# Queries of a latent attention: 18 matmuls per slab step in place of 24, with the weights regathered and the rotation done on VectorE

## The chip, the cores and the metric

The kernel runs on one core of a Trainium2 chip. Its time is the device time of one execution in microseconds (us), the median of three runs where nothing else is said.

## The reference, cut to what matters

The reference is two transformer layers' worth of work, on 256 tokens of width 1024. The part that is changed is the last attention, a latent one with 16 heads. Queries have 64 plain columns ("nope") and 32 columns that are rotated by the token's position ("rope"). All heads share one rotated key of 32 columns.

```
c_q = rmsnorm(xn @ w_dq, cq_norm)                              # 768 wide
q = (c_q @ w_uq).reshape(B, S, 16, 64 + 32)
q = concatenate([q[..., :64], rope(q[..., 64:], positions)])
k = concatenate([k_nope, broadcast(k_rope, 16 heads)])
# rope: out = [x1 * cos - x2 * sin, x1 * sin + x2 * cos]
s = (q . k) / sqrt(96), causal softmax, times v, @ w_o
```

## The kernel before, in words

Everything is kept with features on the partitions and the 256 tokens on the free axis. The weights come as 319 slabs of 128 x 1024 numbers (512 KB), one after the other, through a ring of six slots in SBUF (`stage`). Each slab is split in two: ScalarE copies it to `w_hi` in the reduced format fp32r (`split_hi`, L787), and VectorE subtracts to get the rest, `w_lo` (`minus_hi`, L1141). TensorE then makes three matmuls for each 128 x 128 block: hi by hi, hi by lo, lo by hi (`by_weights`). A slab of eight blocks is 24 matmuls.

Each engine runs its own list of instructions in order, and all of them are written as a loop over the slabs. ScalarE splits slab n + 6 once TensorE has finished slab n (`next_hi`), VectorE splits slab n + 4 at its step n (`next_lo`), and the DMA queue reloads a slot when VectorE has split it. Beside the slabs each engine does in its step n what `attend(n)` gives it: the softmax of the attention heads.

The stage around the change is this. Nine slabs (DQ and KVA) make the latents; at the end of them VectorE rotates the shared key (`k_rope`). Two slabs (UK) make the keys and two (UV) the values. ScalarE's queue then sends the rotated key to all heads by DMA (`rope_keys`). Twelve slabs (UQ) make the queries; I number their steps s = 0 to 11. Eight slabs (MLAO) project the output.

Before the change a head has 128 query columns in UQ: 64 plain, 32 to rotate, and the same 32 with their halves exchanged. One VectorE multiplication by `rQ` takes each head out of PSUM; `rQ` holds the norm's factor, in its lower rows already multiplied by the cosine and the sine. The key carries its rotated 32 rows twice, so the product of 128 rows is the rotated score.

Head g has its scores at the end of step s = 1 + g (`mla_scores`, L594 and after), in steps 1 to 16. After them comes a round trip: VectorE adds the mask and finds the maximum (`maxima`, L1208, L1258), ScalarE takes the exponential (`exps`, L902), VectorE divides by the sum (`probs`, L1264, L1266) as the first thing of its next step, and TensorE transposes the result at the end of that next step (`turned`, L497). ScalarE copies it back (L909). Every second step ends with the product with the values (`outputs`), and its result is taken out by L913 on ScalarE and L1141 on VectorE. In TensorE's list the scores of head g stand ahead of the transposition of head g - 1, and they wait for the maximum of head g - 1.

## Time and profile before

| | |
|---|---|
| median of 3 runs | 1037.84 us (1036.15 to 1038.17) |
| the profiled execution | 1035.64 us, of which the span from first to last instruction is 1033.9 us |
| granted TensorE clock | 0.996 of full speed |
| TensorE busy | 1016.0 us (98%) |
| VectorE busy | 661.0 us (64%) |
| ScalarE busy | 556.8 us (54%) |
| the twelve UQ steps | 749.1 to 798.2 us |

The profile's busy time counts an instruction from its start to its end, and instructions that follow each other closely overlap. So the distance from one start to the next is what an instruction costs in a full queue, and I use that distance below. TensorE's weight loads (PEld) have sharper starts than its matmuls, and I time TensorE by them.

### The profile page before, as it was taken

The numbers are of one execution on the slowest core, as the hardware profiler recorded it, in microseconds if no ns is written. First come the engines' busy times: TensorE is split into PE (matmuls) and PEld (weight loads), VectorE is DVE, ScalarE is ACT, GpSimd is POOL, SyncE is SP. The second block draws the span as 40 slices with busy tenths as digits, with TensorE's granted clock in tenths as the row PEclk, the third lists the DMA queues.
The fourth block names the chain that finished last, engine by engine and source line by source line (L and its number), as shares of the span: only waits on it lengthen the run. The fifth ranks groups of instructions, "written<-read, shape, count | busy, mean of one in ns | idle before, by whom it ended". The sixth has DMA issues, their size and how long they took to land.

```text
span 1033.9 us, 21970 instructions
## 1 busy us (share of the span) xinstructions
PE 1016.0 (98%) x8296; PEld 989.5 (96%) x8296; DVE 661.0 (64%) x1219; ACT 556.8 (54%) x947; POOL 54.7 (5%) x76
## 2 busy tenths in 40 slices
PE   7999999999999999999999999999999999999997
PEld 7999899999999999999999999999999899999996
DVE  5545987775555558666476565648877676565654
ACT  6566786564444446565564444448566564444443
POOL 2021000120000002000010000002100020000000
PEclk9999999999999999999999999999999999999999
DMA  9634344466555555334455555555653445646531
GB/s 342 224 126 143 122 144 159 147 205 197 168 194 172 193 171 181 108 123 145 142 173 183 180 184 180 183 182 166 208 170 109 137 142 185 202 163 200 166 122 41
DMA packets 49208, 172.76 MB, mean 167 GB/s; under 512 B 5376, under 2 KB 7680, under 8 KB 49024
## 3 DMA queue, kind: packets, MB, share of 16 engines
q1 hardware_dynamic: 48096, 170.93, 49.5%
q10 hardware_dynamic: 1056, 1.05, 0.5%
q8 instruction: 39, 0.64, 0.3%
q14 instruction: 17, 0.14, 0.0%
HBM read 169.86 MB, written 1.05 MB: 165 GB/s over the span
## 4 chain that ended last, share of the span: by engine, by line
PE 93%; DVE 4%; ACT 2%; DMA 0%; issue 0%; POOLq 0%; SPq 0%; POOL 0%; ACTq 0%; DVEq 0%
PE bank L307 91%; DVE w_lo L1141 1%; PE bank L497 1%; DVE a_lo L1153 1%; DVE arena_r L1153 1%; DMA xT<-xT_dram 0%; ACT w_hi L787 0%; DVE xT L1170 0%; DVE arena L1134 0%; DVE tmp L1134 0%; ACT L973 0%; DVE arena L1400 0%; ACT soft_p L877 0%; ACT a_hi L827 0%; DVE arena L1388 0%
## 5 line engine op out<-in xcount | busy, mean ns | idle before, releaser
L787 ACT ACTIVATE w_hi<-stage 128x1024 fp32r<-128x1024 f32 x319 | 334.3, 1053 | 189.4 <-PE bank L307 186.0
L307 PE MATMUL bank<-a_hi,w_hi 128*128 128x256 f32 x1488 | 425.6, 287 | 8.2 <-ACT a_hi L987 7.4
L307 PE MATMUL bank<-a_hi,w_lo 128*128 128x256 f32 x1488 | 420.1, 283 | 0.0
L307 PE MATMUL bank<-a_lo,w_hi 128*128 128x256 f32 x1488 | 415.0, 283 | 0.0
L1141 DVE TENSOR_TENSOR w_lo<-stage,w_hi 128x1024 fp32r<-128x1024 f32 x319 | 387.2, 1230 | 10.5 <-ACT w_hi L787 10.3
L307 PE MATMUL bank<-arena_r,w_hi 128*128 128x256 f32 x1840 | 337.1, 285 | 0.8 <-DVE arena_r L1153 0.7
L307 PEld LDWEIGHTS bank<-a_hi,w_hi 128*128 128x128 f32 x1488 | 286.4, 192 | 12.3 <-DVE w_lo L1141 7.9
L307 PEld LDWEIGHTS bank<-arena_r,w_hi 128*128 128x128 f32 x1840 | 286.9, 192 | 2.5 <-DVE arena_r L1153 0.9
L307 PEld LDWEIGHTS bank<-a_hi,w_lo 128*128 128x128 f32 x1488 | 286.4, 192 | 0.0
L307 PEld LDWEIGHTS bank<-a_lo,w_hi 128*128 128x128 f32 x1488 | 283.3, 192 | 1.3 <-issue 1.2
L307 PE MATMUL bank<-arena_r,w_lo 128*128 128x256 f32 x920 | 259.3, 283 | 0.0
L307 PEld LDWEIGHTS bank<-arena_r,w_lo 128*128 128x128 f32 x920 | 176.4, 192 | 0.0
L1134 DVE TENSOR_TENSOR tmp<-bank,rB 128x256 f32<-128x256 f32 x66 | 28.0, 424 | 158.4 <-PE bank L307 158.4
L966 ACT ACTIVATE tmp<-tmp 128x256 f32<-128x256 f32 x66 | 27.6, 417 | 116.0 <-DVE tmp L1134 115.9
L959 ACT ACTIVATE arena_r<-tmp 128x256 fp32r<-128x256 f32 x66 | 27.6, 418 | 97.4 <-DVE tmp L1134 97.4
L1592 POOL TENSOR_TENSOR sumsq<-sumsq,sq 128x256 f32<-128x256 f32 x48 | 38.1, 793 | 718.9 <-ACT sq L813 606.4
L1134 DVE TENSOR_TENSOR tmp<-bank,tmp 128x256 f32<-128x256 f32 x66 | 28.0, 425 | 60.5 <-PE bank L307 60.2
L307 PE MATMUL bank<-w_hi,a_hi 128*128 128x256 f32 x128 | 37.9, 296 | 0.0
L307 PE MATMUL bank<-w_hi,a_lo 128*128 128x256 f32 x128 | 36.7, 287 | 0.0
L307 PE MATMUL bank<-w_lo,a_hi 128*128 128x256 f32 x128 | 36.7, 287 | 0.0
L902 ACT ACTIVATE soft_p<-soft_s,small 128x128 f32<-128x128 f32 x64 | 28.5, 448 | 12.4 <-DVE small L1258 12.1
L1134 DVE TENSOR_TENSOR arena<-bank,rB 128x256 f32<-128x256 f32 x44 | 18.4, 421 | 25.4 <-PE bank L307 25.3
(151 smaller groups left out, 720.5 us busy)
## 6 DMA issues: line engine op xcount, KB each, us to landing
stage<-slab_dram SPq DMA_DIRECT2D x319, 512.0 KB, 3.5
con<-con_dram SPq DMA_DIRECT2D x1, 1153.5 KB, 10.9
xT<-xT_dram SPq DMA_DIRECT2D x4, 256.0 KB, 5.3
arena<-arena ACTq DMA_DIRECT2D x2, 512.0 KB, 7.9
out_dram<-arena SPq DMA_DIRECT2D x8, 128.0 KB, 2.0
vec<-vec_dram SPq DMA_DIRECT2D x1, 245.5 KB, 3.7
pos<-pos_dram SPq DMA_DIRECT2D x1, 128.0 KB, 10.7
```

The lines of the kernel that those rows point to most:

```text
L307: return nc.tensor.matmul(out, lhsT, rhs, start=start, stop=True, skip_group_check=True)
L497: last = nc.tensor.transpose(b[:, i * P:(i + 1) * P], probs[:, i * P:(i + 1) * P], ident)
L787: nc.scalar.activation(w_hi[:, slot, :], stage[:, slot, :], ACT.Copy).then_inc(hi_made, 1)
L902: last = nc.scalar.activation(soft_p[:, g % 2, cols], soft_s[:, g % 2, cols], ACT.Exp, scale=soft_scale(g), bias=s_neg[:, i:i + 1], accum_ ...
L959: nc.scalar.activation(ff_hi[:, c // 2, :], tmp[:, 4 + c // 2, :], ACT.Copy).then_inc(ffhi_ready, 1)
L966: nc.scalar.activation(tmp[:, 2 + p, :], tmp[:, p, :], ACT.Silu).then_inc(silu_ready, 1)
L1134: return nc.vector.tensor_tensor(out, a, b, ALU.mult)
L1141: return nc.vector.tensor_tensor(out, a, hi.bitcast(f32), ALU.subtract)
L1153: return nc.vector.scalar_tensor_tensor(out, x, g, hi.bitcast(f32), ALU.mult, ALU.subtract)
L1592: nc.gpsimd.tensor_tensor(sumsq[:, :], sumsq[:, :], sq[:, (i % 2) * TOK:(i % 2 + 1) * TOK], ALU.add).then_inc(sq_added, 1)
```

## The change

The slabs in DRAM stay as they are, but ScalarE and VectorE read only 96 of the 128 columns of each head. They read three slabs (four heads) as one group, and write the split blocks regathered: the first six blocks of 128 columns hold the 32 rope columns of all four heads, the next six the 64 plain columns of heads 0 and 1, the last six those of heads 2 and 3. A step s is now one such part (`g, part = divmod(s, 3)`), of six blocks.

VectorE takes the rope part out twice for each head, once multiplied by the cosine and once by the sine. ScalarE takes the plain part out by two copies for each pair of heads. The norm's factor is no longer put on the queries; it is the scale of the exponential, one number per token in `rq_col`, and `rq_neg` for the maximum. The key's lower rows hold two different versions of the rotated key, made by eight VectorE instructions in place of four. An empty slab (GAP, 8 columns wide) makes the groups begin at slot 0. Cosine and sine are two tables of 128 rows, so there is one more Sin on ScalarE, in the first feed-forward.

```diff
-UQ = UV + 2
+GAP = UV + 2
+UQ = GAP + 1
...
-        def uq_out(h):
-            return half((4, 0, 1, 2)[h % 4], 0)
+        ROPE_BANK = 4
+
+        def uq_group(t, g):
+
+            return t[:, 3 * (g % 2):3 * (g % 2) + 3, :].rearrange("p s n -> p (s n)")
+
+        def uq_raw(h):
+
+            raw = uq_group(stage, h // 4).rearrange("p (b c) -> p b c", c=P)[:, 6 * (h % 4):6 * (h % 4) + 6, :]
+            return raw[:, :, 0:64], raw[:, :, 64:96]
+
+        def uq_split(t, h):
+
+            blocks = uq_group(t, h // 4)[:, 0:18 * P].rearrange("p (b c) -> p b c", c=P)
+            pair = 6 + 6 * (h % 4 // 2)
+            return (blocks[:, pair:pair + 6, 64 * (h % 2):64 * (h % 2) + 64],
+                    blocks[:, 0:6, 32 * (h % 4):32 * (h % 4) + 32])
...
-            load_rounds(fox + 4, rounds, (0, 1, 2, 3, 4, 5))
+            load_rounds(fox + 4, GAP // SLOTS, (0, 1, 2, 3, 4, 5))
+            for n in range(GAP // SLOTS * SLOTS, UQ):
+                sp.wait_ge(lo_made, n + 1 - SLOTS)
+                cols = slice(0, 8 if n == GAP else SLAB)
+                sp.dma_start(stage[:, n % SLOTS, cols], slab_d[n, :, cols]).then_inc(loaded[n % SLOTS], 16)
+            load_rounds(UQ // SLOTS, rounds, (-1, 0, 1, 2, 3, 4))
...
-                last.then_inc(slab_done, 1)
+                last.then_inc(slab_done, 2 if e == 3 else 1)
...
+                    norm_cols(rQ, latr_ready, 2, bank[7][:, 258:260], latcol_done)
-                n = UQ + s
-                if s == 0:
-                    pe.wait_ge(rope_ready, 1)
-                pe.wait_ge(lo_made, n + 1)
-                for j in range(8):
-                    h, b = divmod(8 * s + j, 6)
-                    if b == 0 and h == 1:
-                        pe.wait_ge(uv_taken, 2)
-                    if b == 0 and h == 3:
-                        pe.wait_ge(uk_taken, 2)
-                    if b == 0 and h >= 4:
-                        pe.wait_ge(uq_taken, h - 3)
-                    last = by_weights(n % SLOTS, j * P, uq_out(h), cq_hi[:, b, :], cq_lo[:, b, :],
-                                      b == 0)
-                last.then_inc(slab_done, 1)
-                attend(n)
+                g, part = divmod(s, 3)
+                if part == 0:
+
+                    pe.wait_ge(lo_made, UQ + 3 * g + 3)
+                    if g:
+                        pe.wait_ge(uq_rope, 4 * g)
+                    else:
+                        pe.wait_ge(rope_ready, 2)
+                    out = half(ROPE_BANK, 0)
+                else:
+
+                    i = 2 * g + part - 1
+                    pe.wait_ge(*((uv_taken, 2), (uv_taken, 2), (uk_taken, 2))[i] if i < 3 else (uq_nope, 2 * i - 4))
+                    out = half(i % 3, 0)
+                for b in range(6):
+                    w = slice((6 * part + b) * P, (6 * part + b + 1) * P)
+                    hi, lo = uq_group(w_hi, g)[:, w], uq_group(w_lo, g)[:, w]
+                    mm(out, hi, cq_hi[:, b, :], b == 0)
+                    mm(out, hi, cq_lo[:, b, :], False)
+                    last = mm(out, lo, cq_hi[:, b, :], False)
+                if part:
+                    last.then_inc(slab_done, part)
+                else:
+                    last.then_inc(uq_rope_done, 1)
+                attend(UQ + s)
...
+            def uq_split_hi(g, heads):
+                act.wait_ge(slab_done, (UK + 2, UV + 2, UQ + 3, UQ + 6)[g])
+                for j in heads:
+                    h, n = 4 * g + j, UQ + 3 * g + (0, 1, 2, 2)[j]
+                    act.wait_ge(loaded[n % SLOTS], 16 * (n // SLOTS + 1))
+                    (nope, rope), (nope_hi, rope_hi) = uq_raw(h), uq_split(w_hi, h)
+                    nc.scalar.activation(nope_hi, nope, ACT.Copy).then_inc(uq_hi, 1)
+                    nc.scalar.activation(rope_hi, rope, ACT.Copy).then_inc(hi_made if j else uq_hi, 1)
...
-                                                scale=soft_scale(g), bias=s_neg[:, i:i + 1],
-                                                accum_out=s_sum[:, i:i + 1])
+                                                scale=0.125 if g < HEADS else rq_col[:, t:t + 1],
+                                                bias=s_neg[:, i:i + 1], accum_out=s_sum[:, i:i + 1])
...
-                            nc.scalar.activation(trig[64:128, :], soft_s[64:128, 0, 0:TOK], ACT.Sin
-                                                 ).then_inc(trig_ready, 1)
+                            nc.scalar.activation(cosine[:, :], soft_s[:, 0, 0:TOK], ACT.Sin).then_inc(trig_ready, 1)
+                            nc.scalar.activation(sine[:, :], soft_s[:, 1, 0:TOK], ACT.Sin).then_inc(trig_ready, 1)
...
-                act.wait_ge(rope_ready, 1)
-                for r in (64, 96):
-                    nc.scalar.dma_start(mla_k[r:r + 32, :, :],
-                                        k_rope[64:96, :].unsqueeze(1).to_broadcast([32, HEADS, TOK])
-                                        ).then_inc(krope_ready, 16)
+                act.wait_ge(rope_ready, 2)
+                nc.scalar.dma_start(mla_k[64:128, :, :],
+                                    k_rope[64:128, :].unsqueeze(1).to_broadcast([64, HEADS, TOK])
...
+                if e:
+                    uq_split_hi(e // 3, ((0, 1), (2, 3), (0, 1))[e - 1])
+            def uq_nope_out(g, part):
+                n, i = UQ + 3 * g, 2 * g + part - 1
+                act.wait_ge(slab_done, n + 2 * part - 1)
+                for e in range(2):
+                    nc.scalar.activation(mla_q[0:64, 2 * i + e, :], half(i % 3, 0)[64 * e:64 * e + 64, :], ACT.Copy
+                                         ).then_inc(uq_nope, 1)
+                for m in range(n + part - 1, n + 2 * part - 1):
+                    next_hi(m)
+
+            uq_split_hi(1, (2, 3))
             for s in range(12):
-                next_hi(UQ + s)
+                if s % 3:
+                    uq_nope_out(*divmod(s, 3))
+                if s in (2, 5):
+                    uq_split_hi(2 + s // 3, (0, 1))
+                if s in (3, 6):
+                    uq_split_hi(1 + s // 3, (2, 3))
                 attend(UQ + s)
...
+            def uq_split_lo(g, heads):
+                for j in heads:
+                    h = 4 * g + j
+                    parts = zip(uq_split(w_lo, h), uq_raw(h), uq_split(w_hi, h))
+                    made = ((uq_hi, 5 * g + (1, 3, 4, 5)[j]), (hi_made, UQ + 3 * g + j) if j else (uq_hi, 5 * g + 2))
+                    for (lo, raw, hi), of in zip(parts, made):
+                        dve.wait_ge(*of)
+                        last = minus_hi(lo, raw, hi)
+                    if j:
+                        last.then_inc(lo_made, 1)
...
+                    times(s_neg[:, i:i + 2], s_max[:, i:i + 2], rq_neg).then_inc(s_taken, 1)
...
-                    times(k_rope[64:96, :], b[64:96, :], trig[64:96, :])
-                    chain(times(tmp[64:96, 0, :], b[96:128, :], trig[96:128, :]))
-                    chain(nc.vector.tensor_tensor(k_rope[64:96, :], k_rope[64:96, :], tmp[64:96, 0, :], ALU.add))
-                    times(k_rope[64:96, :], k_rope[64:96, :], rB[64:96, :]).then_inc(rope_ready, 1)
-                    dve.wait_ge(latr_ready, 1)
-                    dve.wait_ge(trig_signed, 1)
-                    times(rQ[64:128, :], rQ[64:128, :], trig[64:128, :]).then_inc(rq_ready, 1)
-                    dve.wait_ge(rq_ready, 1)
+
+                    own, other, sign = b[64:96, :], b[96:128, :], con[96:128, C_COLS + 2:C_COLS + 3]
+                    for r, of, at, op in ((slice(64, 96), cosine, sine, ALU.add), (slice(96, 128), sine, cosine, ALU.subtract)):
+                        times(k_rope[r, :], own, of[64:96, :])
+                        chain(nc.vector.scalar_tensor_tensor(tmp[r, 0, :], other, sign, at[96:128, :], ALU.mult, ALU.mult))
+                        chain(nc.vector.tensor_tensor(k_rope[r, :], k_rope[r, :], tmp[r, 0, :], op))
+                        times(k_rope[r, :], k_rope[r, :], rB[r, :]).then_inc(rope_ready, 1)
             for e in range(4):
                 next_lo(UK + e)
+                if e >= 2:
+                    uq_split_lo(0, (0, 1) if e == 2 else (2, 3))
...
-                    dve.wait_ge(latcol_done, 1)
+                    dve.wait_ge(latcol_done, 2)
+                    nc.vector.tensor_scalar(rq_col, bank[7][:, 258:260], 96.0 ** -0.5, None, ALU.mult)
+                    nc.vector.tensor_scalar(rq_neg, bank[7][:, 258:260], -96.0 ** -0.5, None, ALU.mult)
                     nc.vector.tensor_copy(r_col[:, :], bank[7][:, 256:258]).then_inc(latcol_ready, 1)
+            def uq_rope_out(g, part):
+
+                dve.wait_ge(uq_rope_done, g + 1)
+                for j in (2 * part, 2 * part + 1):
+                    h, r = 4 * g + j, slice(32 * j, 32 * j + 32)
+                    if h == HEADS - 1:
+                        dve.wait_ge(krope_ready, 16)
+                    times(mla_q[64:96, h, :], half(ROPE_BANK, 0)[r, :], cosine[r, :])
+                    times(mla_q[96:128, h, :], half(ROPE_BANK, 0)[r, :], sine[r, :]).then_inc(uq_rope, 1)
+
+            uq_split_lo(1, (0, 1))
             for s in range(12):
-                n = UQ + s
+                n, (g, part) = UQ + s, divmod(s, 3)
                 attend_first(n)
-                if s < 11:
-                    next_lo(n)
-                dve.wait_ge(slab_done, n + 1)
-                for h in range(8 * s // 6, 8 * (s + 1) // 6):
-                    if h == HEADS - 1:
-                        dve.wait_ge(krope_ready, 32)
-                    times(mla_q[:, h, :], uq_out(h), rQ[:, :]).then_inc(uq_taken, 1)
-                if s == 11:
-                    next_lo(n)
+                if part < 2:
+                    uq_rope_out(g, part)
+                if s == 0:
+                    uq_split_lo(1, (2, 3))
+                if s in (3, 4, 6, 7):
+                    uq_split_lo(1 + s // 3, (0, 1) if part == 0 else (2, 3))
+                next_lo(n)
...```

The order on VectorE in a step of the UQ stage before (s = 4): `w_lo` is a slab's split, `arena<-bank,rQ` takes a head's query out of PSUM, `soft_s` is the mask and maximum, and the reciprocal and `soft_p` are the division.

```order
L1141 TENSOR_TENSOR w_lo<-stage,w_hi 128x1024
L1134 TENSOR_TENSOR arena<-bank,rQ 128x256
L1141 TENSOR_TENSOR arena_r<-bank,arena_r 128x256
L1208 ISA soft_s,small<-bank,con 128x128
L1208 ISA small 128x1
L1208 ISA soft_s,small<-bank,con 128x256
L1208 ISA small 128x1
L1258 TENSOR_SCALAR small<-small 128x2
L1264 RECIPROCAL small<-small 128x2
L1266 TENSOR_SCALAR soft_p<-soft_p,small 128x128
L1266 TENSOR_SCALAR soft_p<-soft_p,small 128x256
```

The same place now, a step with both a rope part and a split of two heads (s = 4). The lines have moved by some 60 to 80 numbers.

```order
L1196 TENSOR_TENSOR arena<-bank,cosine 32x256
L1196 TENSOR_TENSOR arena<-bank,sine 32x256
L1196 TENSOR_TENSOR arena<-bank,cosine 32x256
L1196 TENSOR_TENSOR arena<-bank,sine 32x256
L1203 TENSOR_TENSOR w_lo<-stage,w_hi 128x6x64
L1203 TENSOR_TENSOR w_lo<-stage,w_hi 128x6x32
L1203 TENSOR_TENSOR w_lo<-stage,w_hi 128x6x64
L1203 TENSOR_TENSOR w_lo<-stage,w_hi 128x6x32
L1203 TENSOR_TENSOR arena_r<-bank,arena_r 128x256
L1285 ISA soft_s,small<-bank,con 128x128
L1285 ISA small 128x1
L1285 ISA soft_s,small<-bank,con 128x256
```

Four short multiplications and four short splits stand ahead of the maximum, where one or two multiplications and one slab's split stood.

The order on VectorE ahead of the stage before, from the keys of the second UK slab: `arena<-bank,rKV` takes keys out of PSUM.

```order
L1134 TENSOR_TENSOR arena<-bank,rKV 64x2x256 x4
L1552 COPY r_col<-bank 128x2
L1141 TENSOR_TENSOR w_lo<-stage,w_hi 128x1024
L1134 TENSOR_TENSOR arena<-bank,rKV 64x2x256 x4
L1141 TENSOR_TENSOR w_lo<-stage,w_hi 128x1024 x2
L1134 TENSOR_TENSOR arena<-bank,rQ 128x256
```

The same place now.

```order
L1196 TENSOR_TENSOR arena<-bank,rKV 64x2x256 x4
L1632 TENSOR_SCALAR small<-bank 128x2
L1633 TENSOR_SCALAR small<-bank 128x2
L1634 COPY r_col<-bank 128x2
L1203 TENSOR_TENSOR w_lo<-stage,w_hi 128x6x64
L1203 TENSOR_TENSOR w_lo<-stage,w_hi 128x6x32
L1203 TENSOR_TENSOR w_lo<-stage,w_hi 128x6x64
L1203 TENSOR_TENSOR w_lo<-stage,w_hi 128x6x32
L1196 TENSOR_TENSOR arena<-bank,rKV 64x2x256 x4
L1203 TENSOR_TENSOR w_lo<-stage,w_hi 128x6x64
L1203 TENSOR_TENSOR w_lo<-stage,w_hi 128x6x32
```

The splits of the first group of queries now stand around the second taking of the keys; before, the first query slabs were split earlier and the splits here were for later slabs.

## Rows read from the trace of the kernel before

**Rows 1.** The page, TensorE and VectorE: busy us, share, instructions.

```profile
PE 1016.0 (98%) x8296; PEld 989.5 (96%) x8296; DVE 661.0 (64%) x1219; ACT 556.8 (54%) x947; POOL 54.7 (5%) x76
```

**Rows 2.** The chain that ended last, share of the span by engine.

```profile
PE 93%; DVE 4%; ACT 2%; DMA 0%; issue 0%; POOLq 0%; SPq 0%; POOL 0%; ACTq 0%; DVEq 0%
```

**Rows 3.** Waits of VectorE, 759.5 to 798.2: us, times, longest.

```profile
DVE small L1264 <- ACT soft_p L902: 9.5, 9, 1.1
DVE arena L1134 <- PE bank L307: 0.3, 1, 0.3
```

**Rows 4.** Windows, steps 0 to 2 and 3 to 11: busy us by engine, clock.

```profile
749.10:759.50 10.40, 10.40 (x85) 10.20 (x84) 7.60 (x16) 6.00 (x10) 0.00 (x0) 1.00 0.77 231
759.50:798.20 38.70, 38.70 (x314) 35.98 (x313) 28.24 (x100) 23.58 (x59) 0.00 (x0) 1.00 0.38 123
```

**Rows 5.** Timeline, TensorE's loads: start us, us, what; [idle before].

```profile
749.12 0.41 PEld L307 LDWEIGHTS bank<-arena_r,w_hi 128*128 128x128 f32 x2
...
762.35 0.54 PEld L307 LDWEIGHTS bank<-arena 128*128 128x128 f32 x4
...
771.06 0.54 PEld L307 LDWEIGHTS bank<-arena 128*128 128x128 f32 x4
```

**Rows 6.** Timeline of VectorE, one step of the UQ stage (s = 4).

```profile
766.90 1.22 DVE L1141 TENSOR_TENSOR w_lo<-stage,w_hi 128x1024 fp32r<-128x1024 f32 x1
768.03 0.42 DVE L1134 TENSOR_TENSOR arena<-bank,rQ 128x256 f32<-128x256 f32 x1
768.37 0.41 DVE L1141 TENSOR_TENSOR arena_r<-bank,arena_r 128x256 fp32r<-128x256 f32 x1
768.70 0.28 DVE L1208 CUSTOM_DVE_ANT_0 soft_s<-bank,con 128x128 f32<-128x128 f32 x1
...
769.36 0.17 DVE L1258 TENSOR_SCALAR small<-small 128x2 f32<-128x2 f32 x1
770.59 0.17 DVE L1264 RECIPROCAL small<-small 128x2 f32<-128x2 f32 x1 [1.05 <-ACT soft_p L902]
...
771.25 1.22 DVE L1141 TENSOR_TENSOR w_lo<-stage,w_hi 128x1024 fp32r<-128x1024 f32 x1
```

**Rows 7.** Timeline of VectorE ahead of the UQ stage.

```profile
737.12 0.42 DVE L1134 TENSOR_TENSOR arena<-bank,trig 32x256 f32<-32x256 f32 x1
737.56 0.43 DVE L1134 TENSOR_TENSOR tmp<-bank,trig 32x256 f32<-32x256 f32 x1
...
741.65 0.42 DVE L1502 SCALAR_TENSOR_TENSOR rKV<-bank,arena 128x256 f32<-128x256 f32 x1
743.01 2.79 DVE L1134 TENSOR_TENSOR arena<-bank,rKV 64x512 f32<-64x512 f32 x4 [0.93 <-ACT rKV L802]
745.83 0.16 DVE L1552 COPY r_col<-bank 128x2 f32<-128x2 f32 x1
```

**Rows 8.** Groups of VectorE by shape: busy us, mean ns | idle before.

```profile
L1141 DVE TENSOR_TENSOR w_lo<-stage,w_hi 128x1024 fp32r<-128x1024 f32 x319 | 387.2, 1230 | 10.5 <-ACT w_hi L787 10.3
L1134 DVE TENSOR_TENSOR arena<-bank,rKV 64x512 f32<-64x512 f32 x8 | 5.5, 686 | 1.0 <-ACT rKV L802 0.9
```

**Rows 9.** VectorE's split of wf_split (8 runs of 16): ns min/median/max.

```profile
L1141 DVE TENSOR_TENSOR wf_split<-vec,wf_split x1: 286/286/286, 42.3 to 42.3; 128x128 fp32r<-128x128 f32 x1
```

**Rows 10.** Groups of ScalarE by shape: busy us, mean ns | idle before.

```profile
L840 ACT ACTIVATE arena<-bank,r_col 128x256 f32<-128x256 f32 x16 | 6.7, 471 | 11.8 <-PE bank L307 11.8
L887 ACT ACTIVATE o_raw<-bank 128x256 f32<-128x256 f32 x4 | 1.5, 369 | 0.7 <-PE bank L307 0.7
```

**Rows 11.** Timeline, first feed-forward: the Sin, VectorE's ff_lo, TensorE's next load.

```profile
213.13 0.41 ACT L950 ACTIVATE trig<-soft_s 64x256 f32<-64x256 f32 x1
215.39 0.42 DVE L1141 TENSOR_TENSOR arena_r<-tmp,arena_r 128x256 fp32r<-128x256 f32 x1 [0.48 <-ACT arena_r L959]
215.93 0.31 PEld L307 LDWEIGHTS bank<-arena_r,w_hi 128*128 128x128 f32 x2
```

**Rows 12.** The key's two DMAs, from issue to landing.

```profile
DMA to landing us min/median/max: 6.2/7.9/9.5
```

65 lines of the change are left out of this document (39 added, 26 removed).

## The prediction, made before the changed kernel ran

> **What bounds the kernel now.** I read the page's totals first: TensorE is busy 98% of the span, VectorE 64% [rows 1]. The chain that ended last runs through TensorE for 93% of the span [rows 2]. So a matmul taken away is worth its time only if nothing else moves up to take its place, and that has to be read in the stage that changes. The windows put the twelve UQ steps at 10.4 us for the first three and 38.7 us for the other nine, with TensorE busy all of the time and its clock at full speed [rows 4]. The timeline of TensorE's loads gives the period: from the scores at 762.35 to those two steps later at 771.06 are 8.71 us, 4.36 us a step [rows 5]. In it are 48 matmuls of the two slabs. The first two steps hold nothing else, and from 749.12 to step 2's end I get 0.12 us a matmul; so 5.76 us are slabs and 2.95 us attention.
>
> Then VectorE's list in the same stretch. In 38.7 us it waits for TensorE once, 0.3 us. Its other waits, nine of 1.05 us, are for ScalarE's exponential, which it has itself set off [rows 3]. One step is 766.90 to 771.25, 4.35 us: a split 1.13, a query 0.34, the low part of an output 0.33, then 2.55 from the mask at 768.70 to the end of the division, 1.23 of it between the maximum and the reciprocal [rows 6]. VectorE's share of 64% hides this: here its ordered list takes just as long as TensorE's. TensorE needs each divided head before it can transpose it, so the stage takes the longer of the two lists.
>
> **What the change does to TensorE.** Twelve parts of 18 matmuls stand for twelve slabs of 24: 72 fewer, 72 x 0.12 = 8.6 us. A step pair becomes 36 x 0.12 + 2.95 = 7.27 us, 3.64 us a step, 10.9 us for three. That is the whole gain, if VectorE's three steps take less.
>
> **What it does to VectorE.** The prices first.
>
> A rope multiplication has 32 rows and 256 columns. The trace has one like it before the stage: 0.42 us, and the next begins 0.44 us after it [rows 7]. The 128-row multiplication takes 0.42 as well, with the next 0.34 after it [rows 6]. So fewer rows save nothing, and the next instruction seems to be held. Rows 7 and 8 show the same for the keys: four instructions of 0.686 us in 2.79 us, 0.70 each, where 1024 columns are followed after 1.13 of 1.22 us. I take 0.44, with 0.34 as the other bound. There are 32 of them in place of 16 queries at 0.34. Each pair of heads also holds its two neighbours in the list, 0.08 us twice.
>
> The Trainium skill ("VectorE: DVE Perf Modes", section "Two Vector instructions with no wait between them") speaks against this change: an instruction waits until all earlier Vector ones have finished when an input or its output begins in another group of 32 partitions than the last one in that memory. By it all 32 rope multiplications are held, since cosine and sine results go to rows 64 and 96. The alternating keys agree with it, 0.70 us apart. By the rule the sum is the forecast below; without it, rival 1.
>
> A split: 128 columns took 0.286 us in runs of 16, 512 columns (of another product) 0.686, 1024 took 1.23 [rows 8, 9]. That is a line of 0.153 us and 1/960 us a column, and the short runs lie on it. So 384 columns are 0.55 and 192 are 0.35, each followed 0.08 earlier: 0.47 + 0.27 = 0.74 us a head, 2.96 for four heads against 3.4 for three slabs. If the runs did cost, I bound it by half as much again.
>
> The exponential now has its scale in SBUF. With such a scale 256 columns out of PSUM take 0.471 us, without 0.369 [rows 10]: 0.10 us, two to a head, 0.2 us on each round trip. No row has a scale and a bias of this kind together, so it is 0 to 0.2; I take 0.2.
>
> The Trainium skill ("ScalarE: Activation LUTs", section "What ACT_TABLE_LOAD costs") has each such operand add about 93 ns. By it both would count, 0.19 us a head; if they hid each other it would be nothing.
>
> Now the list, three steps at a time. A softmax turn is 2.55 + 0.2 = 2.75 us.
> Steps 3 to 5: three turns 8.25; eight rope multiplications 3.52 and their neighbours 0.32; four heads' splits 2.96; one low output 0.33. In step 5 VectorE has nothing ahead of the maximum, and ScalarE is late: its exponential stands behind the copy of the head just transposed and behind four splits (two heads, some 1.4 us). I put 0.7. Sum 16.1.
> Steps 6 to 8: the same without the 0.7, with a second low output and the first MLAO slab's split, 1.13: 16.2, and I allow 0.6 for ScalarE, which has a slab's split there. 16.8.
> Steps 9 to 11: 8.25 + 3.84 + three slab splits 3.39 + 0.33 = 15.8.
> Together 48.7 us against TensorE's own 32.7 and against 38.7 before: **10.0 us more**. TensorE gets through its part and then waits for the divided head, or for the maximum that its next scores need.
>
> **The start of the stage.** TensorE could begin at 749.12 [rows 5] plus 0.3 for the new small matmuls of rQ. Now it needs all four heads' splits, because the first part holds all their rope columns. VectorE: eight key instructions of 0.44 from 737.12 are done at 740.7 (four, and one for rQ, before). The empty slab, rKV and the root on ScalarE bring the keys to 742.3; before, from rKV to the keys were 1.36 us [rows 7]. Keys 2.8, three small instructions 0.5, two heads 1.5, keys 2.8, two heads 1.5: 751.4. TensorE begins 2.3 us late. The first part ends at 753.6; the second at 755.7; head 0's scores wait for ScalarE's copy until 756.6. On VectorE the first ropes start at 754.0 and take 1.9 with their neighbours, splits 1.5, ropes 1.8, then head 0's softmax turn 2.75: 761.95. TensorE transposes it and begins step 3 at 762.5, against 759.5: **3.0 us more**.
>
> **The rest.** In the MLAO steps VectorE needs 2.75 + 1.13 + 0.17 = 4.05 us and TensorE 4.36 as before, so the delay neither grows nor is given back. In the first feed-forward the second Sin stands ahead of the silu. VectorE's low part there ends at 215.81 and TensorE loads at 215.93 [rows 11]: nearly no slack, so the Sin's 0.33 us shows as 0.3. The key goes in one DMA, issued at 745.0 instead of 743.3; the slower of the two took 9.5 us [rows 12], so it lands at 754.5, and the first scores come at 756.6: nothing. Two VectorE instructions more for the angles lie beside the WOUT slabs, whose splits run four slabs ahead: nothing.
>
> Sum: 10.0 + 3.0 + 0.3 = 13.3 us. The profiled execution took 1035.64, so 1048.9; it lies 2.2 below the median of the runs, and on the median's scale the forecast is **1051 us**.
>
> **Rivals.**
> 1, the cheap prices: the same wait, but rope multiplications 0.34 apart and no cost of the scale. 24 x 0.10 + 3 x 0.32 + 9 x 0.2 = 5.2 less in steps 3 to 11 and about 1 less at the start: 7 us more than before, 1045. For it: nothing in rows 7 says that it is the rows that hold. Against it: two kinds of instructions at 0.44 and 0.70.
> 2, the other side: TensorE stays the bound and VectorE's additions vanish in its waits for ScalarE. Then 8.6 less, 2.3 for the start and 0.3 for the Sin more: 6 us faster, 1032. It decides once VectorE's three steps are below 10.9 us. They are 16; even with all three round trips taken out (3 x 1.43) about 12 are left. Only rope multiplications at half price could do it, against rows 7.
> 3, the dear prices: strided splits half as dear again, 16 x 0.37 = 6 us, or a key that lands late: 1057. Against it the line through the short runs, and 2 us of slack for the key.
> 4, that the change does little: the saved matmuls and VectorE's additions balance. It needs some 10 us of error in the sum of VectorE's list.
>
> **Chances.** Forecast 60, rival 1 22, rival 2 8, rival 3 7, rival 4 3 in 100. Where slower, the likeliest case alone spans 1048 to 1054. The range, down to most of rival 1 and up to part of rival 3, is 1043 to 1056. Slower by over 0.2% (2 us, about what can be told from no change here) 0.89, within it 0.03, faster 0.08.
>
> **What would show it.** In the changed profile: TensorE idle some 20 us between the KVA slabs and MLAO, released by VectorE's division and maximum, in nearly every step; step 3 beginning some 3 us later; VectorE's rope multiplications 0.44 apart; nine steps at 48 to 49 us; exponentials 0.1 us longer. If the rope multiplications are 0.34 apart it is rival 1. If TensorE shows no waits for VectorE in the stage, the argument is wrong at its root.

## The result, and the profile after

The changed kernel takes 1050.8 us (median of 4 runs, 1048.7 to 1052.64) against 1036.99 us for the kernel before beside it: ratio 1.0136, 95% interval 1.0122 to 1.0150. It is 13.8 us slower; forecast was 1051. The profiled execution has a span of 1049.1 us, 15.2 more than before's.

The page after, busy time by engine, then the chain that ended last by engine; they answer to [rows 1, 2].

```profile
PE 1015.3 (97%) x8228; PEld 983.8 (94%) x8228; DVE 669.7 (64%) x1262; ACT 563.7 (54%) x985; POOL 54.7 (5%) x76
...
PE 86%; DVE 9%; ACT 3%; issue 1%; DMA 1%; SPq 0%; POOLq 0%; POOL 0%; ACTq 0%; DVEq 0%
```

The engines' shares hardly move: 68 fewer matmul records, and still 97% busy. Only the chain tells of the change: VectorE's part is 9% where it was 4%.

Waits of TensorE after, 736 to 840 us: us, times, longest.

```profile
PE bank L328 <- DVE small L1196: 7.1, 7, 2.0
PE bank L518 <- DVE soft_p L1346: 7.0, 8, 1.0
PE bank L328 <- DVE w_lo L1203: 1.5, 1, 1.5
```

These are the forecast's waits: for the maximum (L1196), for the divided head (L1346), and once for the first group's splits, 15.6 us together, where the forecast said some 20.

Windows after: from TensorE's old start of the stage (749.12, moved by the 0.7 us that come ahead of the stage) to step 3, and the nine steps behind it: length, busy us of PE, PEld, DVE, ACT, POOL, granted clock, DMA share, GB/s. They answer to [rows 4].

```profile
749.80:763.10 13.30, 9.78 (x70) 8.50 (x69) 10.80 (x34) 7.83 (x23) 0.00 (x0) 1.00 0.85 260
763.10:813.52 50.42, 37.76 (x260) 31.53 (x259) 34.82 (x118) 29.23 (x81) 0.00 (x0) 0.93 0.28 95
```

TensorE works 37.8 of 50.4 us where it worked 38.7 of 38.7, and its clock is no longer full throughout. VectorE is busy 34.8 us. Of the other 15.6 us it stands 14.1 waiting for ScalarE, with its own work queued behind the wait. It waits for TensorE not once. The waits of VectorE in the second window, which answer to [rows 3]:

```profile
DVE small L1344 <- ACT soft_p L948: 13.0, 9, 2.2
DVE arena_r L1203 <- ACT arena_r L959: 1.1, 1, 1.1
```

The timeline of VectorE after, from the light step 2 (nothing ahead of its maximum) into a heavy one; it answers to [rows 6].

```profile
763.21 0.16 DVE L1196 TENSOR_TENSOR small<-small 128x2 f32<-128x2 f32 x1
765.59 0.17 DVE L1344 RECIPROCAL small<-small 128x2 f32<-128x2 f32 x1 [2.22 <-ACT soft_p L948]
765.79 0.55 DVE L1346 TENSOR_SCALAR soft_p<-soft_p,small 128x128 f32<-128x128 f32 x2
766.37 0.41 DVE L1196 TENSOR_TENSOR arena<-bank,cosine 32x256 f32<-32x256 f32 x1
766.80 0.42 DVE L1196 TENSOR_TENSOR arena<-bank,sine 32x256 f32<-32x256 f32 x1
767.25 0.42 DVE L1196 TENSOR_TENSOR arena<-bank,cosine 32x256 f32<-32x256 f32 x1
767.68 0.42 DVE L1196 TENSOR_TENSOR arena<-bank,sine 32x256 f32<-32x256 f32 x1
768.13 1.56 DVE L1203 TENSOR_TENSOR w_lo<-stage,w_hi 128x384 fp32r<-128x384 f32 x4
769.73 0.29 DVE L1285 CUSTOM_DVE_ANT_0 soft_s<-bank,con 128x128 f32<-128x128 f32 x1
...
771.80 0.17 DVE L1344 RECIPROCAL small<-small 128x2 f32<-128x2 f32 x1 [1.24 <-ACT soft_p L948]
```

The reader is to see three things. The rope multiplications start 0.43 to 0.45 us apart. Two heads' splits take 1.60 from 768.13 to 769.73. The wait for the exponential is 1.24 in place of 1.05, but 2.22 in the light step.

To compare stages I cut each trace at three marks: VectorE's first rotation of the key, TensorE's transposition in step 2, and the one in step 11. All times are us.

| kernel | ratio to before | key to step 2 | nine steps | behind them |
|---|---|---|---|---|
| before | 1 | 21.9 | 38.7 | 236.2 |
| after | 1.0136 | 24.8 | 50.4 | 236.1 |
| e1 no sine | 1.0075 | 23.3 | 45.2 | 236.0 |
| e2 start | 1.0143 | 24.2 | 51.6 | 236.0 |
| e3 before, halves | 1.0079 | 21.9 | 45.1 | 237.0 |
| e4 maximum first | 1.0069 | 24.9 | 41.4 | 236.0 |
| e5 constant scale | 1.0140 | 24.7 | 50.2 | 236.0 |
| e6 same rows | 1.0106 | 24.2 | 48.3 | 236.1 |
| e7 before, maximum first | 1.0005 | 21.9 | 38.8 | 236.7 |
| e8 balanced | 1.0029 | 22.8 | 42.1 | 236.7 |
| e9 even | 0.9999 | 22.8 | 36.7 | 236.9 |
| e10 ScalarE late | 1.0156 | 24.8 | 49.4 | 237.6 |
| e11 deferred | 0.9979 | 22.8 | 36.1 | 236.1 |

After against before: 2.9 us at the start of the stage, 11.7 in the nine steps, nothing behind them, and 0.7 ahead of the key. What comes ahead of the key varies between executions (735.7 to 739.5 us over the runs), so single changes are judged by the columns, whole kernels by the ratio.

### The profile page after: what moved, and what is told of

Its sections match the earlier page's. It is cut to its first block, busy times and chain, and to the rows that moved or that the text cites. A ratio compares the mean times of both kernels' runs of the same rounds, so it can differ in the third digit from the quotient of the medians.

```text
span 1049.1 us, 21879 instructions
## 1 busy us (share of the span) xinstructions
PE 1015.3 (97%) x8228; PEld 983.8 (94%) x8228; DVE 669.7 (64%) x1262; ACT 563.7 (54%) x985; POOL 54.7 (5%) x76
## 3 DMA queue, kind: packets, MB, share of 16 engines
q10 hardware_dynamic: 1040, 1.05, 0.6%
HBM read 169.86 MB, written 1.05 MB: 163 GB/s over the span
## 4 chain that ended last, share of the span: by engine, by line
PE 86%; DVE 9%; ACT 3%; issue 1%; DMA 1%; SPq 0%; POOLq 0%; POOL 0%; ACTq 0%; DVEq 0%
PE bank L328 85%; DVE w_lo L1203 3%; DVE arena L1196 2%; PE bank L518 1%; ACT soft_p L948 1%; DVE a_lo L1230 1%; ACT w_hi L819 1%; DVE arena_r L1230 1%; DMA xT<-xT_dram 1%; DVE soft_s L1285 0%; DVE xT L1247 0%; DVE soft_p L1346 0%; DVE tmp L1196 0%; ACT L1019 0%; DVE arena L1480 0%
## 5 line engine op out<-in xcount | busy, mean ns | idle before, releaser
L328 PE MATMUL bank<-a_hi,w_hi 128*128 128x256 f32 x1488 | 426.0, 287 | 7.8 <-ACT a_hi L1033 7.1
L328 PE MATMUL bank<-a_hi,w_lo 128*128 128x256 f32 x1488 | 420.3, 284 | 0.0
L819 ACT ACTIVATE w_hi<-stage 128x1024 fp32r<-128x1024 f32 x307 | 321.3, 1052 | 175.5 <-PE bank L328 171.8
L328 PE MATMUL bank<-a_lo,w_hi 128*128 128x256 f32 x1488 | 415.3, 284 | 0.0
L1203 DVE TENSOR_TENSOR w_lo<-stage,w_hi 128x1024 fp32r<-128x1024 f32 (+1 forms) x340 | 385.1, 1154 | 11.1 <-ACT w_hi L819 10.5
L328 PE MATMUL bank<-arena_r,w_hi 128*128 128x256 f32 x1792 | 330.6, 286 | 2.3 <-DVE w_lo L1203 1.5
L328 PEld LDWEIGHTS bank<-a_hi,w_hi 128*128 128x128 f32 x1488 | 286.5, 193 | 12.4 <-DVE w_lo L1203 7.6
L328 PEld LDWEIGHTS bank<-a_hi,w_lo 128*128 128x128 f32 x1488 | 286.6, 193 | 0.0
L328 PEld LDWEIGHTS bank<-arena_r,w_hi 128*128 128x128 f32 x1792 | 281.0, 193 | 4.5 <-DVE w_lo L1203 2.0
L328 PEld LDWEIGHTS bank<-a_lo,w_hi 128*128 128x128 f32 x1488 | 283.6, 193 | 1.3 <-issue 1.2
L328 PE MATMUL bank<-arena_r,w_lo 128*128 128x256 f32 x896 | 253.4, 284 | 0.0
L328 PEld LDWEIGHTS bank<-arena_r,w_lo 128*128 128x128 f32 x896 | 172.8, 193 | 0.0
L1196 DVE TENSOR_TENSOR tmp<-bank,rB 128x256 f32<-128x256 f32 x66 | 27.9, 423 | 158.4 <-PE bank L328 158.4
L1012 ACT ACTIVATE tmp<-tmp 128x256 f32<-128x256 f32 x66 | 27.5, 417 | 116.6 <-DVE tmp L1196 116.6
L1196 DVE TENSOR_TENSOR tmp<-bank,tmp 128x256 f32<-128x256 f32 x66 | 28.0, 424 | 60.5 <-PE bank L328 60.3
L948 ACT ACTIVATE soft_p<-soft_s,small 128x128 f32<-128x128 f32 x64 | 31.4, 493 | 25.4 <-DVE small L1196 21.9
L328 PE MATMUL bank<-w_hi,a_hi 128*128 128x256 f32 x128 | 38.1, 297 | 0.0
L328 PE MATMUL bank<-w_hi,a_lo 128*128 128x256 f32 x128 | 36.9, 288 | 0.0
L328 PE MATMUL bank<-arena 64*128 64x256 f32 (+2 forms) x192 | 29.5, 350 | 7.6 <-DVE small L1196 7.1
L328 PE MATMUL bank<-w_lo,a_hi 128*128 128x256 f32 x128 | 36.8, 288 | 0.0
```

What stands on the lines that cost most here:

```text
L328: return nc.tensor.matmul(out, lhsT, rhs, start=start, stop=True, skip_group_check=True)
L819: nc.scalar.activation(w_hi[:, slot, :], stage[:, slot, :], ACT.Copy).then_inc(hi_made, 1)
L948: last = nc.scalar.activation(soft_p[:, g % 2, cols], soft_s[:, g % 2, cols], ACT.Exp, scale=0.125 if g < HEADS else rq_col[:, t:t + 1], b ...
L1012: nc.scalar.activation(tmp[:, 2 + p, :], tmp[:, p, :], ACT.Silu).then_inc(silu_ready, 1)
L1196: return nc.vector.tensor_tensor(out, a, b, ALU.mult)
L1203: return nc.vector.tensor_tensor(out, a, hi.bitcast(f32), ALU.subtract)
```

## The experiments

**e1: without the sine multiplications.**

```diff
-                    times(mla_q[64:96, h, :], half(ROPE_BANK, 0)[r, :], cosine[r, :])
-                    times(mla_q[96:128, h, :], half(ROPE_BANK, 0)[r, :], sine[r, :]).then_inc(uq_rope, 1)
+                    times(mla_q[64:96, h, :], half(ROPE_BANK, 0)[r, :], cosine[r, :]).then_inc(uq_rope, 1)
```

> The changed kernel without the 16 multiplications by the sine: rows 96 to 127 of the queries are never written, everything else stays. Theory (VectorE's ordered list sets the stage, and a multiplication of 32 rows that begins in another group of partitions costs 0.44 us): 16 x 0.44 = 7.0 us less than the changed kernel, 1044, 12 of them in steps 3 to 11 (5.3) and 4 ahead of step 3. Rival with the cheap price, 0.34 apart: 5.4 us less. Rival that TensorE waits for something other than VectorE's list (ScalarE's own work, the splits): within 1 us of the changed kernel.

Measured 1043.21 us, ratio 1.0075 (1.0054 to 1.0097). By the columns 1.6 us less at the start and 5.1 less in the nine steps: 6.7, against 7.0 of the theory and 5.4 of the cheap price. The ratio gives 6.3, with an interval wide enough for both. Time taken out of VectorE's list comes out of the kernel almost one for one.

**e2: the first group split earlier.**

```diff
 # ScalarE
-                if e:
-                    uq_split_hi(e // 3, ((0, 1), (2, 3), (0, 1))[e - 1])
                 if e == 1:
+                    uq_split_hi(0, (0, 1))
                     rope_keys()
+                    uq_split_hi(0, (2, 3))
+                if e == 3:
+                    uq_split_hi(1, (0, 1))
 # VectorE
-                if e >= 2:
-                    uq_split_lo(0, (0, 1) if e == 2 else (2, 3))
+                if e == 2:
+                    uq_split_lo(0, (0, 1, 2, 3))
```

> The changed kernel with all four heads of the first group split earlier: ScalarE splits them in the second of the four key and value slabs, VectorE ahead of the second taking of the keys. TensorE can then begin its first query part 2.5 to 2.8 us earlier. Theory (the start of the stage is VectorE's list too): only VectorE's idle time there goes, 0.26 and 0.68 us in the changed kernel's trace, so 0.6 to 0.9 us less. Rival (what counts is that TensorE begins late): 2.0 to 2.7 us less.

Measured 1051.6 us, ratio 1.0143 (1.0118 to 1.0168): the same as the changed kernel. The start is 0.6 us shorter, as the theory of VectorE's list says and not the rival: TensorE waits for the splits no more, and waits for the maximum instead. But the nine steps are 1.2 us longer, though nothing in them was edited. The windows of 2 us in e2 show why:

```profile
776.00:778.00 2.00, 0.89 (x4) 0.52 (x4) 0.83 (x6) 1.09 (x5) 0.00 (x0) 1.00 0.86 299
778.00:780.00 2.00, 1.08 (x5) 1.09 (x6) 1.43 (x8) 1.98 (x7) 0.00 (x0) 0.55 0.55 225
780.00:782.00 2.00, 2.00 (x12) 2.00 (x11) 0.28 (x2) 1.98 (x8) 0.00 (x0) 0.50 0.00 0
782.00:784.00 2.00, 2.00 (x10) 1.66 (x11) 0.74 (x3) 0.98 (x4) 0.00 (x0) 0.50 0.00 0
```

After a stretch in which TensorE had little to do its granted clock is 0.50, the 1.2 GHz level, for some 6 us. VectorE is nearly idle in the last two windows: here it waits 1.3 us for the slowed TensorE, for which it never waited in the changed kernel's nine steps. The step that ends at 785.61 takes 6.70 us; the same step of the changed kernel takes 4.80.

**e3: the kernel before with two multiplications for one.**

```diff
-                    times(mla_q[:, h, :], uq_out(h), rQ[:, :]).then_inc(uq_taken, 1)
+                    times(mla_q[0:64, h, :], uq_out(h)[0:64, :], rQ[0:64, :])
+                    times(mla_q[64:128, h, :], uq_out(h)[64:128, :], rQ[64:128, :]).then_inc(uq_taken, 1)
```

> The kernel before, in which each query is taken out of PSUM by two multiplications of 64 rows instead of one of 128: the matmuls stay as they are. Theory (VectorE's list is just as long as TensorE's in this stage before the change, and short multiplications that alternate between partitions cost 0.44 each): 2 x 0.44 + 0.08 for the neighbour in place of 0.34, 0.6 us a head, 16 heads: 7 to 10 us more than the kernel before, 1044 to 1047. Rival (TensorE bounds, VectorE has slack): within 1 us of the kernel before.

Measured 1043.89 us, ratio 1.0079 (1.0059 to 1.0098), 8 us more, 6.4 of them in the nine steps. No matmul was touched. The timeline of VectorE in e3, a step with one query:

```profile
770.44 0.85 DVE L1134 TENSOR_TENSOR arena<-bank,rQ 64x256 f32<-64x256 f32 x2
771.33 0.42 DVE L1141 TENSOR_TENSOR arena_r<-bank,arena_r 128x256 fp32r<-128x256 f32 x1
```

The pair takes 0.89 us to the next start; one multiplication took 0.34 [rows 6]. So 0.55 a head, and 12 heads are 6.6 us. VectorE's list had no slack in this stage before the change.

**e4: the maximum ahead of ropes and splits.**

```diff
                 attend_first(n)
+                if s >= 2:
+                    maxima(HEADS + s - 1)
                 if part < 2:
                     uq_rope_out(g, part)
...
-                attend(n)
+                if s < 2:
+                    attend(n)
+                elif n - 3 in MLA_AT:
+                    out_low(MLA_AT[n - 3])
```

> The changed kernel with VectorE's order in steps 2 to 11 changed alone: the mask and maximum come right after the division, ahead of the rope multiplications and the splits, and the low part of an output last. The same instructions all. Theory (the stage is VectorE's list with ScalarE's exponential waited for in each step, 1.2 to 2.2 us): that wait is filled by the ropes and splits, the list shrinks from 50.4 us to about 37, so 12 to 13.5 us less than the changed kernel, 1037.5 to 1039. Rival (the wait only moves: the maximum now waits for TensorE's scores at the end of the step): 5 us less or smaller. Rival (order does not matter, busy time of VectorE alone): 0.

Measured 1042.33 us, ratio 1.0069 (1.0048 to 1.0091). The nine steps are 9.0 us shorter: between the theory's 13 and the rival's 5. By the ratio the kernel wins 6.9. The same instructions in another order are worth at least half of the loss. Why not 13 the timeline of VectorE in a heavy step of e4 shows:

```profile
773.69 1.57 DVE L1203 TENSOR_TENSOR w_lo<-stage,w_hi 128x384 fp32r<-128x384 f32 x4
775.28 0.42 DVE L1203 TENSOR_TENSOR arena_r<-bank,arena_r 128x256 fp32r<-128x256 f32 x1
775.62 0.15 DVE L1344 RECIPROCAL small<-small 128x2 f32<-128x2 f32 x1
```

The exponential had ended at 773.1, but splits and low part stood between, and TensorE waited 2.41 us for this head. I had summed VectorE's list as if TensorE and VectorE could each run at its mean. In the heavy steps VectorE is late, in the light ones it waits, and one does not make up for the other.

**e5: a constant scale.**

```diff
-                                                scale=0.125 if g < HEADS else rq_col[:, t:t + 1],
+                                                scale=0.125 if g < HEADS else 0.01,
...
-                    times(s_neg[:, i:i + 2], s_max[:, i:i + 2], rq_neg).then_inc(s_taken, 1)
+                    nc.vector.tensor_scalar(s_neg[:, i:i + 2], s_max[:, i:i + 2], -0.01, None, ALU.mult).then_inc(s_taken, 1)
```

> The changed kernel, the exponential's scale a constant again and the maximum multiplied by a constant: the norm's factor is left out of the scores. Theory (a scale in SBUF costs 0.10 us in each of the two exponentials of a head, and VectorE's list waits for both): 0.19 us in each of some 11 turns of the stage, 2 us less than the changed kernel, and each turn 2.55 us again in place of 2.73. Rival (the cost is hidden under the bias, or beside the list): 0.

Measured 1051.1 us, ratio 1.0140 (1.0109 to 1.0171): no gain in the time, though the interval is some 3 us to either side and could hide the 2 us of the theory. The wait of VectorE in e5 and in the changed kernel at the same step:

```profile
778.12 0.17 DVE L1344 RECIPROCAL small<-small 128x2 f32<-128x2 f32 x1 [1.05 <-ACT soft_p L948]
```

```profile
778.37 0.17 DVE L1344 RECIPROCAL small<-small 128x2 f32<-128x2 f32 x1 [1.24 <-ACT soft_p L948]
```

The price, 0.19 us a head, is right: seven of the nine steps are 0.17 to 0.19 shorter, 1.25 us in all. The other two are 1.04 longer together. In e5 too the clock is at 0.50 to 0.56 from 778 to 784 us. VectorE waits 1.4 us for TensorE there. So the saving was there, and the clock took it in the profiled execution; for the timed runs that is an inference, with the mean clocks of the last section for it.

**e6: every rope multiplication on the same rows.**

```diff
-                    times(mla_q[64:96, h, :], half(ROPE_BANK, 0)[r, :], cosine[r, :])
-                    times(mla_q[96:128, h, :], half(ROPE_BANK, 0)[r, :], sine[r, :]).then_inc(uq_rope, 1)
+                    q = slice(0, 32)
+                    times(mla_q[64:96, h, :], half(ROPE_BANK, 0)[q, :], cosine[q, :])
+                    if h >= 6:
+                        dve.wait_ge(uq_rope, h - 5)
+                    times(tmp[64:96, h % 6, :], half(ROPE_BANK, 0)[q, :], sine[q, :]).then_inc(uq_rope, 1)
```

The expectation names rows 64 to 95 as input too; what ran reads rows 0 to 31 and writes rows 64 to 95, always the same.

> The changed kernel, every rope multiplication with rows 64 to 95 as input and output (the sine's result goes to a scratch tile, so the queries' rotation is wrong). As many instructions of the same size. Theory (what costs 0.44 instead of 0.34 is the change of the group of partitions from one to the next): inside a part the four multiplications are 0.34 apart, 3 x 0.10 in each of 8 parts, 2.4 us less than the changed kernel. Rival (it is the small number of rows that costs): 0.44 apart, no change.

Measured 1047.07 us, ratio 1.0106 (1.0080 to 1.0132); start and nine steps are 2.7 us shorter (forecast 2.4). The timeline of VectorE in e6:

```profile
752.54 0.42 DVE L1196 TENSOR_TENSOR arena<-bank,cosine 32x256 f32<-32x256 f32 x1 [0.67 <-PE bank L328]
752.88 0.40 DVE L1196 TENSOR_TENSOR tmp<-bank,sine 32x256 f32<-32x256 f32 x1
753.21 0.41 DVE L1196 TENSOR_TENSOR arena<-bank,cosine 32x256 f32<-32x256 f32 x1
753.54 0.41 DVE L1196 TENSOR_TENSOR tmp<-bank,sine 32x256 f32<-32x256 f32 x1
753.98 1.56 DVE L1203 TENSOR_TENSOR w_lo<-stage,w_hi 128x384 fp32r<-128x384 f32 x4
```

The same instructions are 0.33 to 0.34 us apart, and only the last, ahead of one that begins in other rows, is 0.44. It is the change of rows that costs, not their small number.

**e7: the kernel before, maximum first.**

```diff
                 attend_first(n)
+                if s >= 2:
+                    maxima(HEADS + s - 1)
                 if s < 11:
                     next_lo(n)
```

> The kernel before with the order of e4: VectorE takes the mask and maximum right after the division in steps 2 to 11, ahead of the slab's split and the queries. Theory (before the change TensorE's list is as long as VectorE's, so a shorter VectorE list alone gives nothing): within 1 us of the kernel before. Rival (the round trip through ScalarE was what set the stage before too): 2 to 6 us less. Second rival (with the order changed VectorE waits for TensorE's scores with the splits behind it, and TensorE for the splits): slower by 2 us or more.

Measured 1037.89 us, ratio 1.0005 (0.9992 to 1.0019): no difference. In the waits of VectorE in e7, 736 to 840 us, the time it has won is a wait for TensorE's scores:

```profile
DVE soft_s L1208 <- PE bank L307: 10.9, 11, 2.0
DVE small L1264 <- ACT soft_p L902: 6.3, 6, 1.1
```

With e3 this closes the account of before: its two lists were equally long, so lengthening VectorE's costs at once and shortening it alone gives nothing.

**e8: balanced.**

```diff
+                if s in (5, 8):
+                    uq_split_lo(g + 1, (2, 3))
...
+                if s >= 2:
+                    maxima(HEADS + s - 1)
                 if part < 2:
                     uq_rope_out(g, part)
-                if s == 0:
-                    uq_split_lo(1, (2, 3))
-                if s in (3, 4, 6, 7):
-                    uq_split_lo(1 + s // 3, (0, 1) if part == 0 else (2, 3))
+                if s in (3, 4, 6, 7):
+                    uq_split_lo(g + 1, (part,))
+                if s == 1:
+                    maxima(HEADS)
+                    uq_split_lo(1, (2, 3))
```

> The changed kernel with e4's order and four things more. VectorE's splits of two heads stand one at a time behind the ropes of the first two steps of a group and two ahead of the maximum of the third; the first group's heads are split as in e2; head 0's maximum stands ahead of the splits of the second group; ScalarE's splits stand behind its exponential; the two Sin behind the silu. In e4 TensorE still waited 8.5 us for the divided heads, 2.4 and 2.7 us each where both ropes and a pair of splits stood between maximum and division, while in the third step of a group VectorE idled 1.5 us for ScalarE and 1.5 us for TensorE. Theory (it is the distance in the list from maximum to division that counts): 6 to 9 us less than e4, 1033 to 1036, about the kernel before or below. Rival (the work, not its place, is too much): 2 us less than e4 or nothing.

Measured 1039.7 us, ratio 1.0029 (1.0014 to 1.0043), 4 us less than e4 by the ratio, not 6 to 9. The diff shows the main of VectorE's part; the rest is in the expectation. In the profiled execution the start is 2.1 us shorter (24.9 to 22.8), but the nine steps are 0.7 longer (42.1) and so is what comes behind them, so it explains little of the 4 us; it took 1041.21, 1.5 over the median of this kernel. TensorE waited 1.67 us for a divided head and 1.16 for the pair of splits, and its clock was at 0.50 from 776 to 778 us. The step that ends at 779.50 took 6.67.

**e9: spread evenly.** Against e8, VectorE's splits alone:

```diff
-                if s in (5, 8):
-                    uq_split_lo(g + 1, (2, 3))
+                if 3 <= s < 9:
+                    uq_split_lo(g + 1, (part + 1,))
...
-                if s in (3, 4, 6, 7):
-                    uq_split_lo(g + 1, (part,))
+                if s in (2, 5):
+                    uq_split_lo(g + 2, (0,))
```

The single splits, the low part and two slabs' splits now stand between division and maximum.

> e8 with VectorE's splits spread once more. In e8's trace TensorE waited 1.7 us where a split and a low part stood between maximum and division, and 1.2 and 1.1 us for the splits of two heads at the start of a group. Now only the ropes (in the first two steps of a group) or one head's split stand between maximum and division; the other splits, one head a step, stand between the division and the next maximum, where VectorE waited for TensorE's scores. ScalarE splits one head ahead of its exponential and one behind it. Sum of VectorE's list in steps 3 to 11: 11.7 + 12.9 + 11.9 = 36.5 us against 38.7 in the kernel before and some 42 in e8. Theory (the place in the list counts, and the list is now near its bare work): 3 to 5 us less than e8, 1034.5 to 1037, the same as the kernel before or a little less. Rival (the maximum comes late instead, behind the splits): the same as e8. Rival (TensorE's clock falls after its waits, as in the changed kernel's trace, and takes 1 to 2 us): 1038.

Measured 1036.01 us, ratio 0.9999 (0.9987 to 1.0010): the same as the kernel before. The nine steps are 36.7 us, the list's sum was 36.5. The clock is 1.00 in all of them, and the step that took 6.67 in e8 takes 4.44: part of what e9 wins over e8 in the profiled executions is the clock. The 2.0 us won against the kernel before in the nine steps are given back by 0.8 at the start and 0.7 behind them.

**e10: ScalarE's splits behind its exponential.**

```diff
+                attend(UQ + s)
                 if s in (2, 5):
                     uq_split_hi(2 + s // 3, (0, 1))
                 if s in (3, 6):
                     uq_split_hi(1 + s // 3, (2, 3))
-                attend(UQ + s)
```

> The changed kernel with ScalarE's order alone changed: in each step of the stage its splits stand behind its exponential instead of ahead of it. Theory (what the forecast of the nine steps missed is that ScalarE is late three times; in the changed kernel's trace VectorE waits 2.22 and 2.07 us for an exponential instead of 1.24, and 1.09 for an output's high part): up to 2.9 us less than the changed kernel, and each wait of VectorE for an exponential 1.24 us. Rival (ScalarE's splits then come late to VectorE's, which stand behind the next maximum): 0 to 1 us less.

Measured 1052.07 us, ratio 1.0156 (1.0138 to 1.0173): no gain. The waits of VectorE shrink less than expected (2.22 to 1.48, 2.07 to 1.82, the third is gone), and the nine steps by 1.0 us. The shorter waits are 2.1 us together, but some 1.2 come back. VectorE waits 0.19 for a slab's high part, and 0.99 for a rope part of TensorE:

```profile
784.33 0.42 DVE L1197 TENSOR_TENSOR arena<-bank,cosine 32x256 f32<-32x256 f32 x1 [0.99 <-PE bank L328]
```

TensorE's clock was at 0.53 and 0.62 in the two windows before, 780 to 784 us. Then 1.5 us go behind them, where nothing was edited. The windows of e10 at the end of the stage:

```profile
812.00:814.00 2.00, 0.99 (x6) 0.59 (x7) 0.83 (x4) 2.00 (x6) 0.00 (x0) 1.00 0.56 217
814.00:816.00 2.00, 2.00 (x13) 2.00 (x12) 1.82 (x6) 1.10 (x4) 0.00 (x0) 0.56 0.04 8
816.00:818.00 2.00, 2.00 (x12) 2.00 (x12) 0.72 (x3) 2.00 (x6) 0.00 (x0) 0.59 0.85 252
```

The clock is down where the output projection begins, and there TensorE is the bound: nothing hides it.

**e11: two slabs' splits deferred.** Against e9:

```diff
-                if s in (9, 11):
-                    next_lo(UQ + {9: 9, 11: 10}[s])
...
-                    next_lo(n)
+                    next_lo(UQ + {8: 8, 11: 9}[s])
 # rows_out, for the output projection alone
-                    if n < base + NC - 2:
+                    if base == MLAO:
+                        for m in {5: (3, 4), 6: (5,)}.get(n - base, (n - base - 2,) if n < base + 5 else ()):
+                            next_lo(base + m)
+                    elif n < base + NC - 2:
                         next_lo(n)
```

> e9 with two of the output slabs' four splits (1.13 us each) taken out of VectorE's list in steps 9 to 11 and made up in the sixth and seventh step of the output projection, where the heads are done and VectorE waits. In e9's trace TensorE waits 0.77 and 0.82 us for the divided heads in steps 10 and 11 and VectorE's list of steps 9 to 11 is 0.6 us longer than TensorE's. Theory (VectorE's list still sets the stage): 1 to 2 us less than e9, 1034.2 to 1035.2, just below the kernel before. Rival (TensorE is the bound again in these steps, or the slabs that follow come late): as e9 or more.

Measured 1034.81 us, ratio 0.9979 (0.9969 to 0.9990): 2.2 us faster than the kernel before, at the edge of what can be told. The waits of TensorE in e11, 736 to 840 us:

```profile
PE bank L518 <- DVE soft_p L1351: 3.1, 4, 1.2
PE bank L328 <- DVE w_lo L1208: 0.4, 2, 0.2
```

Of 15.6 us of waits for VectorE in the changed kernel 3.5 are left. The nine steps are 36.1 us, where TensorE alone would need 32.7.

## Why the prediction was right

The mechanism was right and the total too, 13.3 us forecast against 13.8 between the medians. In the profiled executions the difference is 15.2, so the terms were somewhat low. That the total came so close is in part luck: the sum of the nine steps holds two slips of its own, told below, that nearly cancel.

**TensorE's saving, 8.6 us.** The matmuls went, but the time turned into waits. Only with other orders could part of it be had: e9's nine steps are 2.0 us below before's.

**The nine steps, 10.0 forecast, 11.7 measured.** The prices held: ropes 0.44 [rows 7] (shown by e1 and e6), splits 1.60 for two heads against 1.48 and a neighbour's 0.08, the scale 0.19 a head (e5). The sum did not. Steps 6 to 8 add up to 16.8, not "16.2": 15.4 for steps 3 to 5 without the 0.7, then 0.33 and 1.13. And TensorE's nine steps go with VectorE's steps 2 to 10, not 3 to 11: its list ends there with the division of step 11, so the slab's split of that step, 1.13, stands outside, and the light step 2 inside. Put right, the same prices give 48.2 us, 9.5 more than before.

The term that was mis-sized is ScalarE's lateness, "I put 0.7" and "I allow 0.6". It was late three times: 2.22 (step 2) and 2.07 (step 5) in place of 1.24, and 1.09 (step 8) for an output's high part, which stood behind two slabs' splits. That is 2.9 us together against 1.3: 1.6 of the 2.2 us between 48.2 and the measured 50.4. Step 2 alone, for which the sum had nothing, is 1.0 of it. The other 0.6 are small errors of the prices. e10 took only 1.0 of the lateness away, since the clock fell and VectorE had to wait for TensorE instead.

**The start, 3.0 forecast, 2.9 measured.** TensorE began at 752.20 instead of 749.12, counted from the key's rotation 2.4 us later (forecast 2.3). But TensorE's late beginning was not the cause: e2 removed it and won 0.6. VectorE's list was: e1 took four multiplications out of it there and won 1.6. Its order is part of that: e8 and e9, which have e2's edit too, put head 0's maximum ahead of four splits and won 2.1 together.

**The Sin, 0.3 forecast.** The timeline of ScalarE after, first feed-forward, answers to [rows 11]:

```profile
213.70 0.42 ACT L996 ACTIVATE cosine<-soft_s 128x256 f32<-128x256 f32 x1
214.03 0.40 ACT L997 ACTIVATE sine<-soft_s 128x256 f32<-128x256 f32 x1
214.34 0.40 ACT L1012 ACTIVATE tmp<-tmp 128x256 f32<-128x256 f32 x1
```

TensorE's load behind it moved from 215.93 to 216.61. But 0.58 of that was there before the Sin: a split of ScalarE that began at 209.94 begins at 210.52, and it does so in e3 too, where nothing is edited here. So the Sin cost 0.1.

**The key's transfer and the output projection, nothing forecast.** One transfer, 8.5 us to landing, no wait; behind the nine steps 236.1 us against 236.2.

**The rivals.** Rival 1 (ropes 0.34 apart) would need e6's spacing in the changed kernel; it has 0.44. Rival 2 (TensorE stays the bound) falls with e1 and e3: VectorE's list alone moves the time. Rival 3's dear splits are not there: 384 columns took 0.554 us, 192 took 0.350, as the line through the short runs had it.

## What to carry to other kernels

When an engine is 98% busy and another 64%, compare their ordered lists in the stage that changes, with every round trip in them: a list with waits can be just as long as a full one, and then work moved off the busy engine lands on the bound. Count the pieces by what the next instruction's start is put off, and look at whether neighbours change partitions. Before such a change is given up, look at what stands in the list between a result and the instruction that waits for it: here the order of VectorE's and ScalarE's lists was worth 14 us (e9), as much as the whole loss.
